# First and last cell of an output projection as eight plain products, its subtractions on VectorE and its squares on ScalarE

## The reference

```python
x = x + jnp.concatenate([o_a, o_m, o_b], axis=-1) @ w_out          # 2048 -> 2048
up = rmsnorm(x, g_ffn) @ w_up                                      # 2048 -> 12288
up, f_conv_new = causal_dwconv(up, f_conv_past, conv_f_w, conv_f_b)
val, gt = jnp.split(up, 2, axis=-1)
x = x + (jax.nn.gelu(gt) * val) @ w_down                           # 6144 -> 2048
```

## Time and profile before

| | us |
|---|---|
| median of 3 runs | 2331.01 (2329.01 to 2331.37) |
| profiled execution, its own time | 2330.44 |
| span in its profile | 2328.7 |
| output projection, from its first product (588.80) to the end of the first cell of w_up's sixth product (825.67) | 236.87 |

### The profile page before, as it was taken

The page is one execution under the profiler, slowest core; times in us unless marked ns, Lnnn a source line. Parts: engine busy times, 40 slices in busy tenths (PEclk is TensorE's granted clock), DMA queues, the critical chain, the costliest instruction groups (busy, mean ns, idle before and its releaser), DMA issues.

```text
span 2328.7 us, 44834 instructions
## 1 busy us (share of the span) xinstructions
PE 2287.8 (98%) x17808; PEld 2266.5 (97%) x17808; DVE 1899.3 (82%) x2467; ACT 1184.4 (51%) x1900; POOL 415.5 (18%) x280
## 2 busy tenths in 40 slices
PE   9999999999799799999999999999999999999999
PEld 8999999999799799999999999999999999999999
DVE  6778666665999988888888888888888988787876
ACT  4566454454444555555545555555555555454643
POOL 5100000000455811112112111121111010000000
PEclk9999999999899899999999999999999999999999
DMA  9433333332255153434344434344344678686864
GB/s 294 147 82 85 101 90 93 100 88 83 71 170 155 55 135 116 134 117 137 117 122 126 125 117 134 117 134 123 111 135 135 181 195 203 162 212 154 216 147 103
DMA packets 479605, 309.87 MB, mean 133 GB/s; under 512 B 11176, under 2 KB 457640, under 8 KB 479416
## 3 DMA queue, kind: packets, MB, share of 16 engines
q1 hardware_dynamic: 470984, 289.97, 42.3%
q0 software_dynamic: 8432, 17.27, 4.5%
HBM read 255.79 MB, written 53.51 MB: 133 GB/s over the span
## 4 chain that ended last, share of the span: by engine, by line
PE 60%; DVE 2%; issue 1%; DMA 1%; ACT 0%; POOL 0%; SPq 0%; DVEq 0%; ACTq 0%; POOLq 0%
PE out L2889 20%; PE out L2890 20%; PE out L2891 20%; DVE ring_l L2263 1%; DMA out_yT<-stage 0%; DVE fl L2491 0%; DMA h_forms<-fb 0%; ACT ring_h L1587 0%; DVE out L2367 0%; DVE s_buf L2276 0%; DVE pair L2303 0%; DVE pair L2296 0%; DVE pair_d L2296 0%; ACT fh L1746 0%; DVE ub L2323 0%
## 5 line engine op out<-in xcount | busy, mean ns | idle before, releaser
L2263 DVE TENSOR_TENSOR ring_l<-pair,ring_h 128x1024 fp32r<-128x1024 f32 (+1 forms) x384 | 458.8, 1195 | 176.3 <-ACT ring_h L1587 176.1
L1587 ACT CAST ring_h<-pair 128x1024 fp32r<-128x1024 f32 (+1 forms) x384 | 383.3, 998 | 319.9 <-DVE pair L2296 224.9
L2889 PE MATMUL out<-t,ring_h 128*128 128x272 f32 x1792 | 519.8, 290 | 19.8 <-DVE ring_l L2164 7.1
L2891 PE MATMUL out<-t,ring_l 128*128 128x272 f32 x1792 | 518.0, 289 | 0.0
L2890 PE MATMUL out<-t,ring_h 128*128 128x272 f32 x1792 | 517.5, 289 | 0.0
L2889 PE MATMUL out<-b,ring_h 128*128 128x272 f32 x1344 | 390.8, 291 | 13.5 <-DVE ring_l L2263 6.4
L2889 PE MATMUL out<-fh,ring_h 128*128 128x272 f32 x1344 | 387.9, 289 | 3.0 <-DVE ring_l L2263 2.1
L2891 PE MATMUL out<-b,ring_l 128*128 128x272 f32 x1344 | 389.8, 290 | 0.0
L2890 PE MATMUL out<-b,ring_h 128*128 128x272 f32 x1344 | 389.6, 290 | 0.0
L2890 PE MATMUL out<-fl,ring_h 128*128 128x272 f32 x1344 | 386.9, 288 | 0.0
L2891 PE MATMUL out<-fh,ring_l 128*128 128x272 f32 x1344 | 384.9, 286 | 0.0
(11 more groups left out here) (299 smaller groups left out, 4108.8 us busy)
## 6 DMA issues: line engine op xcount, KB each, us to landing
pair<-in_w_up SPq DMA_DIRECT2D x192, 512.0 KB, 4.0
raw<-in_w_in SPq DMA_DIRECT2D x36, 1024.0 KB, 5.6
pair<-in_w_down SPq DMA_DIRECT2D x64, 384.0 KB, 4.4
pair_d<-in_w_down SPq DMA_DIRECT2D x64, 384.0 KB, 4.5
h_forms<-fb SPq DMA_DIRECT2D x24, 816.0 KB, 6.1
fr<-h_forms SPq DMA_DIRECT2D x24, 816.0 KB, 6.6
out_yT<-stage POOLq DMA_DIRECT2D x31, 544.0 KB, 8.1
pair<-in_w_out SPq DMA_DIRECT2D x28, 512.0 KB, 4.6
```

The lines of the kernel that those rows point to most:

```text
L1587: nc.scalar.copy(ring_h[:, n % 3, 0:width(i)], weight_of(p, i)).then_inc(op_hi, 1)
L2263: v.tensor_tensor(ring_l[:, n % 3, 0:w], weight_of(p, i), ring_h[:, n % 3, 0:w].bitcast(F32), ALU.subtract).then_inc(op_lo, 1)
L2889: mm(out, w_high, high[:, k, :], start=opens and k == 0, stop=False, skip_group_check=True)
L2891: ins = mm(out, w_low, high[:, k, :], start=False, stop=k == tiles - 1, skip_group_check=True)
```

## The change

Cell 0 and cell 7 of the output projection are no longer done in seven products but in eight: for each plain weight quarter (order 0, 2, 1, 3) one product with the left half of the rows and one with the right. Quarters 0 and 2 multiply B11 and T1, quarters 1 and 3 multiply B21 and B22; since T1 = B12-B11, the product with B11 is added to the right half as well (in cell 0 from a copy that `keep_o` makes of it, in cell 7 out of PSUM by `add_last`). Such a cell needs no S and neither T2, T3 nor T4, which are now first read in cell 1 and last in cell 6. One cast and one low part of the weights then serve two products (4 instead of 7 in such a cell).

GpSimd does only the additions of the squares of tiles 0 to 13. T1 to T4 (both for w_out and x1), S3 of each cell and of the first w_up cell, and the two low parts move to VectorE; the squares move to ScalarE (`activation(Square)`); the last two are added on VectorE. T1 of the first seven heads is formed during the last head's attention. The first forms of x1 (B11, T1, B21) take the places of T2, T3 and T4 of w_out (`x1_form`), which cell 7 no longer reads. The mean's matmul moves behind the seventh product of the first w_up cell. All counts of `product` go through `done()`, since one weight slot now serves up to two products. The places of w_down's forms in SBUF are renumbered, with the same sizes.

```diff
+def plain_at(q, d):
+    return (len(O_QUARTERS) + PROD * O_SUMS if d else 0) + O_QUARTERS.index(q)
...
+        mix_form = {1: v11, 2: v21, 3: v22, 5: x_1, 7: x_2, 4: x_3, 6: x_4}
+        x1_form = {6: v11, 4: v21, 3: v22, 7: x_1, 5: x_2, 2: x_3, 1: x_4}
...
-            nc.gpsimd.tensor_tensor(b12, b12, b11, ALU.subtract).then_inc(mix_t, 1)
...
-            def square_x1(k):
...
-                    nc.gpsimd.tensor_tensor(sq1[:] if k else sum1[:], tile, tile, ALU.mult
-                                            ).then_inc(x1_squared, 1)
...
+            for k in range(KT - 2):
+                sum_x1(k)
...
+            def square_x1(k, dst):
+
+                tile_complete(act, k)
+                nc.scalar.activation(dst[:], rows[:, k, :], ACT.Square).then_inc(x1_squared, 1)
+
+            def square_early(k):
+
+                if k:
+                    act.wait_ge(sums_x1, k)
+                square_x1(k, sq1 if k else sum1)
...
+            def mix_t1(first, end, heads):
+
+                dve.wait_ge(flip_read, flips_before(HM + heads))
+                v.tensor_tensor(right(first, end), right(first, end), left(first, end), ALU.subtract).then_inc(mix_t, 1)
...
+            def make_o_s3(d):
+
+                dve.wait_ge(s2_made, d)
+                dve.wait_ge(op_lo, o_at(5, d) + 1)
+                v.tensor_tensor(o_quarter(d, 2), o_quarter(d, 3), o_quarter(d, 0), ALU.subtract).then_inc(s3_made, 1)
...
+            def multiply_plain(q, p, d):
+
+                if d == 0:
+                    pe.wait_ge(xlo, KT + {1: 1, 5: 4, 2: 5, 3: 6}[p])
+                    if (q, p) == (0, 1):
+                        pe.wait_ge(mixed, RT - 1)
...
+                n = plain_at(q, d)
+                pe.wait_ge(op_lo, n + 1)
+                opens = q in (0, 2) or (d > 0 and p == 2)
+                block(plain_banks(d)[q, p], n % 3, *mix_form[p], K8, opens).then_inc(product, 1)
...
+            def plain_cell(d):
+                for q in O_QUARTERS:
+                    for p in (2, 3) if q % 2 else (1, 5):
+                        multiply_plain(q, p, d)
+
+            plain_cell(0)
+            for d in range(1, O_LAST):
+                for p in O_ORDER:
                     multiply_o(p, d)
+            plain_cell(O_LAST)
...
             for p in ORDER_FIRST:
                 multiply(p, 0)
-                if p == 7:
-                    pe.wait_ge(sums_x1, KT)
-                    mean(N_X1ROWS, mean_rows[:], sum1)
+            pe.wait_ge(sums_x1, KT)
+            mean(N_X1ROWS, mean_rows[:], sum1)
             multiply(1, 1)
```

More of the change, by code:

```diff
@@ L898, in load_form @@
                     old, last = divmod(n - SLOTS_D, PROD)
[L899 removed]
+                    sp.wait_ge(product, done(at(USES[last], FT + PAIRS_D * (old + 1) - 1)))
                 elif n == SLOTS_D - 1:
@@ L1592, in keep_a @@
                     return
-                act.wait_ge(product, at(1, i) + 1)
+                act.wait_ge(product, done(at(1, i)))
                 if i == 0:
@@ L1600, in keep_b @@
             def keep_b(i):
-                act.wait_ge(product, at(6, i) + 1)
+                act.wait_ge(product, done(at(6, i)))
                 if i:
@@ L1630, in read_c21 @@
             def read_c21(i):
-                act.wait_ge(product, at(4, i) + 1)
+                act.wait_ge(product, done(at(4, i)))
                 if i < FT:
@@ new lines, in _ @@
+                if d == O_LAST - 1:
+                    act.wait_ge(product, done(o_at(6, d)))
+                    act.wait_ge(x1_scaled, K8)
+                    hi_x1(x1_form[1][0], left(0, K8))
+                hi_o(4, d)
+                if d == 2:
+                    scale_x1(2)
+                    scale_x1(3)
+                if d < O_LAST - 1:
+                    hi_o(1, d + 1)
+                    hi_o(5, d + 1)
+            d, e, last = O_LAST, EARLY, KT - 1
+            hi_plain(0, d)
@@ new lines, in _ @@
+            act.wait_ge(product, done(o_at(7, d - 1)))
+            act.wait_ge(x1_t, 1)
+            hi_x1(x1_form[5][0], right(0, K8))
+            hi_plain(2, d)
+            hi_plain(1, d)
+            square_early(last - 3)
+            square_early(last - 2)
+            scale_x1(last - 3)
+            scale_x1(last - 2)
+            act.wait_ge(x1_scaled, K8 + e)
+            hi_x1(x1_form[2][0][:, 0:e, :], left(K8, K8 + e))
+            hi_plain(3, d)
+            act.wait_ge(product, plain_product(2, 1, d))
@@ L2227, in add_o @@
             def add_o(p, d):
-                dve.wait_ge(product, o_at(p, d) + 1)
+                dve.wait_ge(product, done(o_at(p, d)))
                 if p == 1:
@@ L2339, in read_c12 @@
             def read_c12(i):
-                dve.wait_ge(product, at(3, i) + 1)
+                dve.wait_ge(product, done(at(3, i)))
                 if i >= FT:
@@ L2456, in _ @@
-            lo_op(4, 0)
-            lo_x1(10, bl[2][:, e:K8, :], right(K8 + e, KT), bh[2][:, e:K8, :])
+            dve.wait_ge(x1_squared, KT)
+            for k in range(2):
+                dve.wait_ge(sums_x1, last - 1 + k)
+                v.tensor_tensor(sum1[:], sum1[:], sq_late[k][:], ALU.add).then_inc(sums_x1, 1)
+            dve.wait_ge(sums_x1, KT)
+            lo_x1(10, x1_form[3][1][:, 0:e, :], right(K8, K8 + e), x1_form[3][0][:, 0:e, :])
+            lo_x1(12, x1_form[3][1][:, e:K8, :], right(K8 + e, KT), x1_form[3][0][:, e:K8, :])
@@ L2562, in _ @@
             lo_op(3, g)
-            dve.wait_ge(product, at(7, g) + 1)
+            dve.wait_ge(product, done(at(7, g)))
             dve.wait_ge(last_kept, 2)
@@ L2922, in multiply_o @@
-                opens = p in (1, 2, 5) or (d == 0 and p in (3, 4))
-                block(out, n % 3, *forms[p], K8, opens).then_inc(product, 1)
-            for d in range(O_CELLS):
-                for p in O_ORDER if d else O_FIRST:
+                block(out, n % 3, *mix_form[p], K8, p in (1, 2, 5)).then_inc(product, 1)
+            def plain_cell(d):
+                for q in O_QUARTERS:
+                    for p in (2, 3) if q % 2 else (1, 5):
+                        multiply_plain(q, p, d)
@@ L2953, in multiply @@
                 if i < FT:
-                    high, low = forms[p]
+                    high, low = x1_form[p]
                 else:
```

635 lines of the change are left out of this document (309 added, 326 removed).

## The result

The changed kernel takes 2296.82 us (median; 2295.11 to 2300.33, 4 runs) where the kernel before takes 2330.01 (2328.91 to 2331.37, 4 runs): a ratio of 0.9859, 95% interval 0.9842 to 0.9876, or 33.2 us less. The forecast was 2299.5 us in a range of 2290 to 2311. The profiled execution took 2295.11 us with a span of 2293.3, which is 35.4 under the span of before.

The account below looks back on a forecast made before the run. The prediction took TensorE, busy 98% of 2328.7 us, to bound the kernel. From 2330.44 us, +6.0 - 20.0 - 1.4 - 15.6 = -31.0 gave 2299.4, stated as 2299.5 us, in a range of 2290 to 2311.

Parts of the forecast that it names:

- Two more products: Output projection: two extra products on TensorE at 3.01 us each, hidden by nothing, +6.0 us.
- Entry: Start of the output projection: no product waits any more, so the 20.0 us lost there go.
- Cells: Cells 1 to 6 of the projection: 1.0 of the 2.4 us lost is left, -1.4 us.
- Exit: Projection's end and w_up's first cell: losses fall from 27.1 to 11.5 us, -15.6 us.
- Wait (a): Exit, products 4 and 3 of w_up's first cell: TensorE waits 4.0 us for VectorE (bounds 1.6 and 6).
- Wait (b): Exit, behind the mean: TensorE idles 3.1 us for root, cast and low part of the second cell's product 1.
- two slow products: Exit: a product at slow clock behind each of the two waits left, 2 x 2.2 us, 4.4 in all.
- The rest at 0: w_up's rest and w_down: same instructions at other addresses, change of 0.
- Clock stays up: Rival: the exit's two waits bring no slow product, 2293 us, or a gap is missed, 2295; chance 0.14 together.
- Stalls come back: Rival: one or two TensorE stalls return at entry or exit, 2305 to 2311 us; chance 0.18.
- VectorE full: Rival: VectorE's busy time is work, so the entry's loss stays and grows by 9.3, 2329 us; chance 0.03.
- squares hold the casts: Rival: squares on ScalarE hold up the weights' casts and TensorE, slower, up to 2341 us; chance 0.04.

Follow-up runs that it names:

- e6: The changed kernel with the entry's subtractions T1 to T4 back on GpSimd, plain cells kept: 2308.95 us.
- e10: The changed kernel with the entry's T1 to T4 on GpSimd, T2 to T4 each cut into eight operations: 2307.88 us.
- e4: The changed kernel with the squares of tiles 0 to 13 of x1 back on GpSimd: 2300.11 us.
- e11: The changed kernel with the squares of tiles 0 to 13 of x1 back on GpSimd, run a second time: 2300.96 us.
- e1: The changed kernel with the mean moved ahead of product 3 of w_up's first cell: 2292.32 us.
- e9: The changed kernel with the root queued on ScalarE behind the casts of the second w_up cell's products 1 and 2: 2295.81 us.
- e8: The kernel before with only the entry's T1 to T4 and first S2 and S3 on VectorE, cell 0 still in seven products: 2322.15 us.
- e5: The changed kernel itself, unchanged, measured once more: 2297.03 us.
- e2: The changed kernel with the last two additions of x1's squares on GpSimd in place of VectorE: 2296.44 us.
- e7: The changed kernel with the six subtractions for x1's forms at the exit back on GpSimd: 2307.31 us.
- e3: The changed kernel with the mean ahead of product 3 and the last two additions of squares on GpSimd: 2291.27 us.

## Why the prediction was right, point by point

*Two more products, +6.0.* 63 products take 189.97 us in one piece, 3.01 each: as forecast.

*Entry, -20.0.* No product of the first nine waits or is slow: as forecast. T1's low part was ready 2.8 us ahead of the second product, for a forecast margin of 2.9. The mechanism, VectorE held and not full, is shown by e6 and e10. My reading of the Trainium skill's "Perfetto Trace Analysis" (Optimizing Scalar/DVE Operations) stands: its first half, which would move work off a busy VectorE, costs 11.9 us here, and its caution on the shared port is what the rows show.

*Cells, -1.4.* They gave all 2.4. I had left 1.0 for GpSimd's two additions in each cell; they cost nothing in this trace. e4 and e11 say that in the changed kernel the squares on ScalarE are worth 3 to 4 us, more than the 2.4 that the cells of before lost; my sum had no term for what they would cost if they stayed.

*Exit, -15.6.* Wait (a) was forecast at 4.0 with product 3's weights 22.1 us behind the end of cell 7. It was 0.75 and 3.32, together 4.07. The weights were there at 21.9 and product 3 began at 22.4: some 0.4 of the wait is the read of C22, which my sum didn't have. Wait (b) was 3.09, forecast 3.1, with the chain as named; e1 and e9 show that it hangs on the mean's and the root's places. The term that was mis-sized is "two slow products": 4.4 forecast, 1.6 measured in the first profile (0 and 1.6) and 2.9 in the repeat (1.3 and 1.6). Counted as the prediction counts, by the length of the stretch less 3.01 for each product and 0.7 for the mean, 9.8 were left, 11.0 in the repeat, not 11.5. That is the waits of 7.2, the slow clock of 1.6 and 1.0 of small things: the last matmul's end ahead of each wait, a slower start behind it, and 0.2 more for the mean.

*The rest at 0.* The projection started 0.8 earlier; in the executions of this study its first product starts between 587.92 and 588.94, whatever the kernel. The tail behind the exit took about 0.9 less, but it is two differences of opposite sign. From the fourth product behind the mean (the second cell of w_up) to w_down's first product it is 970.11 us before and 971.15, 971.16 and 971.16 in the changed kernel, its repeat and e1: 1.0 longer, though TensorE never idles there. Matmuls come every 125.1 ns in before and in e8, every 125.3 in the changed kernel, e1 and e11, so this one comes with the kernel; its cause is open, and the prediction had 0. w_down then takes 516.02 where before took 517.85; some 1.4 of that is its pace, which changes by execution (below).

Together, against the span: +6.0 - 20.0 - 2.4 - 17.3 - 0.8 - 0.9 = -35.4. The median fell by 33.2, since the profiled run was the fastest of its four. So small terms part the forecast from the result: 1.0 in the cells, 1.7 at the exit (0.5 in the repeat), 0.8 at the start and 0.9 in the tail. The clock at the exit, the start and w_down's pace change by execution, so that the time came so near is in part luck; that the waits stand where they were named is not.

*Rivals.* "Clock stays up" was half true, once, and by chance of the execution. "Stalls come back" and "VectorE full" are refuted by the first window, "squares hold the casts" too: two squares in each cell, and TensorE never idle. "Stalls come back" had 2.8 us of room at the second product.

## What to carry to other kernels

When VectorE looks nearly full, look at how long one shape takes at its shortest and at its longest before calling it work: 1.22 against 5.82 us for the same shape meant here that it stood behind a GpSimd operation, and then *moving work from GpSimd to VectorE* took less of VectorE's time than leaving it. A recursion that saves products is worth its price only where its forms can be ready; at the entry one more product of 3.0 us, in a cell that reads what is there, took away the 12 us that the engine alone had left (e8). For the last cell this is argued and not shown. And look last at what is queued ahead of the first operation behind a reduction: moving one mean by one product was worth 4.7 us more.

## What the runs showed of the hardware

Whether the clock falls behind a wait of TensorE isn't settled by the wait's length alone. Behind the wait of 3.3 us before product 3 the clock was 1.00 in the first profile, e4 and e10, and 0.66, 0.65, 0.63 and 0.50 in e5, e9, e11 and e6. Behind the 3.09 after the mean it was 0.84 to 0.86 over three products in the first profile, e2, e4, e5, e6 and e10, 0.74 in e7, and 1.00 in e11 alone:

```profile
788.33:792.94 4.61, 4.61 (x24) 4.61 (x25) 0.24 (x1) 0.00 (x0) 0.00 (x0) 0.63 0.73 187
797.11:806.40 9.29, 9.29 (x72) 9.09 (x72) 8.88 (x7) 3.08 (x5) 2.41 (x1) 1.00 0.01 2
```

So such a wait costs 0 to 2.9 us on top (e7), mostly 1.3 to 1.6, by the execution. In e7 the clock was 0.65 over product 3 behind a wait of 2.03, in e1 it was 1.00 behind one of 2.40. The Trainium skill's "TensorE: Matmul & The Clock Gate" (What's actually happening) has the gate look in windows that don't go in step with the kernel; e5 beside the first profile agrees.

w_down runs at one of two paces. The same kernel, the squares on GpSimd, in its first and its second profile, on two chips:

```profile
1910.00:2010.00 100.00, 100.00 (x803) 100.00 (x802) 77.03 (x94) 49.58 (x75) 7.20 (x6) 1.00 0.72 173
```

```profile
1910.00:2010.00 100.00, 100.00 (x806) 100.00 (x805) 77.77 (x94) 50.24 (x75) 8.40 (x7) 1.00 0.72 174
```

Matmuls come every 124.8 or every 124.4 ns, start to start, without a gap. Both paces stand on each of two chips (e1, e2, e4 slower and e3 faster on one; e6 slower and e5, e7 faster on the other), so neither the kernel nor the chip sets it alone. From w_down's first matmul to its last it is 517.4 us in e1, e2, e4 and e6 and 516.0 to 516.2 in the changed kernel, e3, e5, e7, e9, e10 and e11: 1.3 us of scatter. What sets it is open.

The hold between VectorE and GpSimd goes both ways: 6.62 us for a GpSimd addition that takes 1.83 at its median elsewhere, while VectorE's operations followed each other without a pause.
